# Three score banks, and a new order of exponentials, copies, rotations and maxima, in the attention of a hybrid encoder step

## The reference, cut to what matters

```python
q_lat = jnp.einsum('bthn,chn->bthc', q[..., :MLA_NOPE], lw['w_uk'])
s = jnp.einsum('bqhc,bkc->bhqk', q_lat, ckv) + jnp.einsum('bqhr,bkr->bhqk', q_pe, kpe)
s = s.astype(jnp.float32) * MLA_SCALE
mask = (k_pos[None, :] // CHUNK) <= (q_pos[:, None] // CHUNK)      # CHUNK = 64
s = jnp.where(mask[None, None], s, jnp.finfo(jnp.float32).min)
p = jax.nn.softmax(s, axis=-1).astype(ckv.dtype)
o = jnp.einsum('bhqk,bkc->bqhc', p, ckv)
```

## Time and profile before

| what | value |
|---|---|
| median of three runs | 2607.68 us |
| the profiled execution: its time, its span | 2606.66 us, 2604.8 us |
| TensorE busy | 2562.2 us (98%) |
| VectorE, ScalarE, GpSimd busy | 1644.5, 1137.5, 532.3 us |
| prompt attention, first layer | 617.5 to 700.5 us of the span |
| prompt attention, second layer | 1901.3 to 1984.5 us |
| mean granted TensorE clock | 0.999 |

### The profile page before, as it was taken

One profiled execution on the slowest core, in us unless ns is written; L12 is line 12 of the kernel. 1 busy time (PEld: TensorE's weight loads), 2 busy tenths in 40 slices (PEclk: granted clock), 3 DMA queues, 4 the chain that ended last, 5 costly groups with the idle time before them and its releaser, 6 DMA issues.

```text
span 2604.8 us, 44565 instructions
## 1 busy us (share of the span) xinstructions
PE 2562.2 (98%) x17872; PEld 2446.6 (94%) x17872; DVE 1644.5 (63%) x2566; ACT 1137.5 (44%) x1922; POOL 532.3 (20%) x440
## 2 busy tenths in 40 slices
PE   8999999999999999999999999999999999999998
PEld 8999999996689999999999999999956899999998
DVE  5666575646466866657577574765564757757473
ACT  5343344424654534334454342553165535434253
POOL 0010112103754101011210110121066441101011
PEclk9999999999999999999999999999999999999999
DMA  3322324220025122232313222334100161322231
GB/s 116 91 81 81 97 65 113 73 59 11 20 54 100 49 82 81 84 95 71 108 33 96 83 71 76 89 89 105 27 11 30 46 130 34 97 81 71 85 85 59
DMA packets 369794, 190.73 MB, mean 73 GB/s; under 512 B 38541, under 2 KB 365536, under 8 KB 369630
## 3 DMA queue, kind: packets, MB, share of 16 engines
q1 hardware_dynamic: 365248, 177.89, 25.3%
q0 software_dynamic: 4000, 10.47, 1.8%
q10 hardware_dynamic: 382, 0.14, 0.0%
HBM read 182.53 MB, written 5.93 MB: 72 GB/s over the span
## 4 chain that ended last, share of the span: by engine, by line
PE 90%; DVE 4%; POOL 2%; ACT 2%; issue 1%; DMA 1%; SPq 0%; DVEq 0%; POOLq 0%; ACTq 0%
PE ps L734 27%; PE ps L735 27%; PE ps L736 27%; PE ps L1111 2%; POOL misc L3201 1%; POOL qkc L3204 1%; PE ps L1122 1%; PE ps L1223 1%; DVE at L2696 1%; PE ps L1224 1%; PE ps L1154 0%; PE ps L1245 0%; PE ps L1173 0%; ACT css L1536 0%; PE ps L1236 0%
## 5 line engine op out<-in xcount | busy, mean ns | idle before, releaser
L734 PE MATMUL ps<-xh,w 128*128 128x320 f32 x1920 | 595.3, 310 | 2.8 <-DVE css L2961 2.8
L736 PE MATMUL ps<-xh,w 128*128 128x320 f32 x1920 | 593.5, 309 | 0.0
L735 PE MATMUL ps<-xl,w 128*128 128x320 f32 x1920 | 593.4, 309 | 0.0
L1536 ACT ACTIVATE w<-raw 128x512 fp32r<-128x512 f32 (+3 forms) x372 | 315.8, 861 | 484.2 <-PE ps L736 466.2
L3058 POOL TENSOR_TENSOR hl<-ub,hh 128x640 fp32r<-128x640 f32 x88 | 174.1, 1978 | 1448.4 <-ACT hh L1536 1381.3
L734 PE MATMUL ps<-hh,w 128*128 128x320 f32 x1408 | 438.1, 311 | 3.3 <-DVE ub L2352 1.2
L735 PE MATMUL ps<-hl,w 128*128 128x320 f32 x1408 | 435.2, 309 | 0.0
L736 PE MATMUL ps<-hh,w 128*128 128x320 f32 x1408 | 435.2, 309 | 0.0
L734 PEld LDWEIGHTS ps<-xh,w 128*128 128x128 f32 x1920 | 360.4, 188 | 4.9 <-DVE css L2961 3.2
L735 PEld LDWEIGHTS ps<-xl,w 128*128 128x128 f32 x1920 | 360.4, 188 | 0.3
L736 PEld LDWEIGHTS ps<-xh,w 128*128 128x128 f32 x1920 | 360.4, 188 | 0.0
(11 more groups left out here) (418 smaller groups left out, 4671.2 us busy)
## 6 DMA issues: line engine op xcount, KB each, us to landing
raw<-in_w_ffn_in_dram SPq DMA_DIRECT2D x176, 512.0 KB
raw<-in_w_ffn_out_dram SPq DMA_DIRECT2D x192, 192.0 KB
raw<-in_w_in_dram SPq DMA_DIRECT2D x38, 512.0 KB
raw<-in_w_ffn_out_dram SPq DMA_DIRECT2D x64, 128.0 KB
wraw<-in_w_out_dram SPq DMA_DIRECT2D x8, 512.0 KB
raw<-in_w_out_dram SPq DMA_DIRECT2D x8, 512.0 KB
out_dram<-xio SPq DMA_DIRECT2D x5, 512.0 KB
xin<-in_x_prompt_dram SPq DMA_DIRECT2D x4, 512.0 KB, 7.6
```

Of the source, the lines that this page charges most:

```text
L734: pe.matmul(out, wh, xh, start=first, stop=False, skip_group_check=loose)
L735: pe.matmul(out, wh, xl, start=False, stop=False, skip_group_check=loose)
L736: return pe.matmul(out, wl, xh, start=False, stop=last, skip_group_check=loose)
L1536: return nc.scalar.activation(out, in_, func, **kw)
```

## The change

The scores get a third PSUM bank, taken in the order 3, 4, 2. The latent queries move out of bank 2 into the end of bank 1, and the rotary queries beside them, as two matmuls of 64 columns on different rows instead of one of 128, with two copies on ScalarE instead of one. The scores of a head's tile 3 are made one step earlier, and those of the next head's tile 1 and 2 too; tile 0 of the next head stays where it was. ScalarE does the exponential of tile n + 2 ahead of the copy of tile n + 1, but for each head's step i = 2, where the old order stays. VectorE takes a head's last maximum ahead of the rotation of the next head's second half, which stood before it; the gate steps stay ahead of the maximum of their tile.

```diff
--- before.py
+++ after.py
@@ -597,6 +597,10 @@
         w = 2 * LEVELS[n]
         return ap.rearrange("p (n q) -> p n q", q=w)[:, :, w // 2:w]
 
+    def scores_of(n):
+
+        return PS[:, (3, 4, 2)[n % 3], :]
+
     def level_end(n):
 
         return sum(k <= n for k, _ in LEVEL_STEPS)
@@ -1137,9 +1141,11 @@
             pe.wait_ge(*q_ready.nth(l, 2 * h + 1))
             if h:
                 pe.wait_ge(*ql_sb.nth(l, h - 1))
-            pe.matmul(PS[:, 2, 0:P], WUKT[:, h, :], QT[0:NOPE, h % 2, TP:T], start=True, stop=True)
-            pe.matmul(PS[0:ROPE, 1, HALF:HALF + P], PAIR, QT[NOPE:P, h % 2, TP:T], start=True, stop=True)\
-                .then_inc(ql_ps.sem, 1)
+            pe.matmul(PS[:, 1, HALF:HALF + P], WUKT[:, h, :], QT[0:NOPE, h % 2, TP:T], start=True, stop=True)
+            for e in range(2):
+                mm = pe.matmul(PS[ROPE * e:ROPE * e + ROPE, 1, HALF + P:512], PAIR,
+                               QT[NOPE:P, h % 2, TP + 64 * e:TP + 64 * e + 64], start=True, stop=True)
+            mm.then_inc(ql_ps.sem, 1)
 
         def attend_scores(l, n):
             h, i = divmod(n, PT_)
@@ -1149,9 +1155,11 @@
                 pe.wait_ge(*kt_sb.nth(l, h))
                 if h == 0:
                     pe.wait_ge(*kt_rope.nth(l, 0))
-            if n >= 2:
-                pe.wait_ge(*exp_sb.nth(l, n - 2))
-            pe.matmul(PS[:, 3 + n % 2, 0:(i + 1) * P], QT[:, h % 2, i * P:(i + 1) * P],
+            if n >= 3:
+                pe.wait_ge(*exp_sb.nth(l, n - 3))
+            elif n == 2:
+                pe.wait_ge(*kt_sb.nth(l, 1))
+            pe.matmul(scores_of(n)[:, 0:(i + 1) * P], QT[:, h % 2, i * P:(i + 1) * P],
                       KT[:, h % 2, 0:(i + 1) * P], start=True, stop=True).then_inc(s_ps.sem, 1)
 
         def attend_transpose(l, n):
@@ -1250,6 +1258,7 @@
             mla_prep(l)
             attend_scores(l, 0)
             attend_scores(l, 1)
+            attend_scores(l, 2)
             pe.wait_ge(*cn_sb.nth(l, 0))
             head_queries(l, 1, 0)
             head_latents(l, 0)
@@ -1258,8 +1267,10 @@
                 h, i = divmod(n, PT_)
                 if i == 1 and h + 1 < H:
                     head_queries(l, h + 1, 1)
-                if n + 2 < NT:
+                if n + 2 < NT and i == 2:
                     attend_scores(l, n + 2)
+                if n + 3 < NT and i != 1:
+                    attend_scores(l, n + 3)
                 if i == 0 and h % 2 and h + 1 < H:
                     pair_keys(l, h // 2 + 1)
                 if i == 2 and h + 2 < H:
@@ -1884,9 +1895,11 @@
 
             def latent_queries(h):
                 act.wait_ge(*ql_ps.nth(l, h))
-                run(QLAT[:, :, h, :], PS[:, 2, 0:P].rearrange("p (b t) -> p b t", t=TS), ACT.Copy)
-                run(QPE[0:ROPE, :, h, :], PS[0:ROPE, 1, HALF:HALF + P].rearrange("p (b t) -> p b t", t=TS), ACT.Copy)\
-                    .then_inc(ql_sb.sem, 1)
+                run(QLAT[:, :, h, :], PS[:, 1, HALF:HALF + P].rearrange("p (b t) -> p b t", t=TS), ACT.Copy)
+                for e in range(2):
+                    ins = run(QPE[0:ROPE, 4 * e:4 * e + 4, h, :],
+                              PS[ROPE * e:ROPE * e + ROPE, 1, HALF + P:512].rearrange("p (b t) -> p b t", t=TS), ACT.Copy)
+                ins.then_inc(ql_sb.sem, 1)
 
             def probabilities(n):
                 h, i = divmod(n, PT_)
@@ -1895,7 +1908,7 @@
                     act.wait_ge(*t_ps.nth(l, n - 2))
                 if i == 0 and h > 3 and h % 2 == 0:
                     act.wait_ge(*rs_sb.nth(l, h // 2 - 2))
-                run(PB[:, n % 2, 0:(i + 1) * P], PS[:, 3 + n % 2, 0:(i + 1) * P], ACT.Exp,
+                run(PB[:, n % 2, 0:(i + 1) * P], scores_of(n)[:, 0:(i + 1) * P], ACT.Exp,
                     bias=MX[:, n % 4, 1:2], accum_out=SUMS[:, h // 2 % 2, i, h % 2:h % 2 + 1]).then_inc(exp_sb.sem, 1)
 
             def transposed(n):
@@ -1970,11 +1983,13 @@
                     head_queries(h + 1, 1)
                 if i == 0 and h:
                     latent_queries(h)
+                if n + 2 < NT and i != 2:
+                    probabilities(n + 2)
                 if n + 1 < NT:
                     transposed(n + 1)
                 if n % 8 == 2 and n > 8:
                     pair_rows(n // 8 - 1)
-                if n + 2 < NT:
+                if n + 2 < NT and i == 2:
                     probabilities(n + 2)
                 if i == 0 and h % 2 and h + 1 < H:
                     head_keys(h + 1)
@@ -2657,8 +2672,8 @@
                 i = n % PT_
                 dve.wait_ge(*s_ps.nth(l, n))
 
-                chain.link(V.memset(PS[0:64, 3 + n % 2, i * P + 64:(i + 1) * P], -FAR))
-                V.reduce_max(MX[:, n % 4, 1:2], PS[:, 3 + n % 2, 0:(i + 1) * P], AX_X, negate=True)\
+                chain.link(V.memset(scores_of(n)[0:64, i * P + 64:(i + 1) * P], -FAR))
+                V.reduce_max(MX[:, n % 4, 1:2], scores_of(n)[:, 0:(i + 1) * P], AX_X, negate=True)\
                     .then_inc(nm_sb.sem, 1)
 
             def inverse_sums(pair):
@@ -2787,9 +2802,9 @@
                     gate_ends_exponents()
                 if n == 16:
                     gate_negative()
+                maximum(n)
                 if n % PT_ == PT_ - 1 and n // PT_ + 1 < H:
                     rotated(n // PT_ + 1, 1)
-                maximum(n)
                 if n % PT_ == 0 and n // PT_ + 1 < H:
                     rotated(n // PT_ + 1, 0)
                 if n % 8 == 1 and n > 8:
```

## The result

The changed kernel is slower: 2611.80 us median (2609.59 to 2614.34, 20 runs) against 2607.34 us (2605.45 to 2608.74, 20 runs) on the same chip, a recorded ratio of 1.0019 with a 95% interval of 1.0012 to 1.0025 (the two medians alone give 1.0017). I had forecast 2607.2 us and 2603.2 to 2610.5. The profiled execution took 2609.59 us, its span is 2607.8 us, and its mean granted clock 0.998 (before: 0.999).

The account below looks back on a forecast made before the run. GpSimd's chain from ScalarE's copy qt to the streams' first matmul bounds the stage; two layers at 0.2 us plus 0.1 slack save 0.5, so 2606.2 profiled, 2607.2 us median, range 2603.2 to 2610.5.

Parts of the forecast that it names:

- GpSimd's start: Attention stage: GpSimd's differences start when ScalarE copies qt at n = 5, forecast 0.2 us earlier in each layer.
- the copy of tile 3: ScalarE's copy of tile 3's transposes, ahead of qt: forecast to start at 628.2 instead of 628.75, 0.55 us earlier.
- tile 6's exponential: On ScalarE ahead of qt: forecast 0.55 us earlier, still waiting for its maximum, as it did 1.49 us.
- tile 5's copy: ScalarE's 0.36 us copy, formerly inside the exponential's wait, now behind it; reduces the 0.55 us gain to 0.2.
- the parts without a price: Extra rotary matmuls and copies, and the reorderings: assumed free under waits; could remove up to TensorE's 4.1 idle us.
- GpSimd's chain: From GpSimd's start to the streams' first matmul: 63.2 us, with no step that the change edits.
- wait for kn: TensorE's wait ahead of the streams' first matmul: forecast to grow from nothing visible (first layer) to 2 or 3 us.
- (B): GpSimd's taps fall ahead of VectorE's scans and qt comes earlier: 1.5 to 2.4 us a layer, 2603 to 2604.6; chance 0.15.
- Rival (C): Copies stand behind exponentials awaiting late maxima, delaying GpSimd's second wait: 2616, or 2610.4 at half; chance 0.17 in all.
- The port: GpSimd's first tap against VectorE's scan: tap first gains 1.3 us, scan first loses 0.3; no change taken.
- Rival (A): TensorE's order decides the stage, so its idle time counts: 2591 if all went, 2599.5 with 4.1 us; chance 0.07.
- Rival (D), the clock: TensorE arrives up to 4.1 us early, stands still and the granted clock falls: 2610.6 us; chance 0.06.

Follow-up runs that it names:

- banks_rotation: Changed kernel with the exponential back behind the copy at every step; third bank, earlier scores and last maximum ahead of rotation kept: 2608.27 us.
- section 3: Experiments moving GpSimd's gate-row stores ahead of its last four taps (changed kernel 2611.94 us, kernel before 2606.21), or using the exponential's new place only late.
- taps_out_after: Changed kernel without the second and third convolution tap on GpSimd (8 of 12 taps left out, result differs): 2603.38 us.
- banks_only: Changed kernel with both new orders undone; third score bank, moved latent queries and earlier scores alone: 2611.02 us.
- late_taps_after: Changed kernel, whole computation, GpSimd's tap 1 only behind the second differences, then clears and stores, tap 2, cache loads, tap 3: 2622.19 us.
- tap1_out_after: Changed kernel without tap 1 of the convolution (4 of GpSimd's 12 taps, beside the first gate steps): 2605.03 us.
- filler_after: Changed kernel with four filling matmuls of 256 columns ahead of the transposes at n = 3 to 9: 2613.42 us.
- stores_first_after: Changed kernel with GpSimd's clears of QPE and two gate-row stores ahead of its last four taps: 2611.94 us.
- taps_early_after: Changed kernel, whole computation, with GpSimd's differences and taps 1 and 2 each allowed to begin one head earlier: 2615.70 us.
- late_exponential: Changed kernel with the exponential ahead of the copy only from step n = 15 on: 2608.63 us.
- late_exp_stores_first: Changed kernel with the exponential ahead only from n = 15 on and GpSimd's stores ahead of its last four taps: 2608.66 us.
- banks_exponential: Changed kernel with the last maximum back behind the rotation; banks and exponential ahead of the copy kept: 2616.05 us.
- orders_only: Kernel before, with two score banks and its own score order, plus both new orders (exponential ahead of copy, maximum ahead of rotation): 2620.71 us.
- filler_before: Kernel before with four filling matmuls of 256 columns ahead of the transposes at n = 3 to 9: 2615.71 us.
- stores_first_before: Kernel before with GpSimd's clears and gate-row stores ahead of its last four taps: 2606.21 us.

## Why the prediction was wrong

**What held.** GpSimd's start 0.2 us earlier (20.28 to 20.09 us into the stage). The steps behind it too: the copy of tile 3 was to come 0.55 us earlier and came 0.49 earlier (11.22 to 10.73 into the stage), tile 6's exponential waits 1.60 us where I had left the 1.49, and tile 5's copy of 0.38 us stands behind it, as worked out. In the second layer the first tap was in front of the scan, which I had left open. The extra passes and copies cost nothing measurable in banks_rotation, which has them all.

**What failed: the parts without a price.** The step is "The earlier scores, the exponentials ahead of copies, and the last maximum ahead of the rotation from n = 6 on can remove up to the 4.1 us of TensorE's idle time, but they end in a longer wait for kn, since GpSimd is late." I took GpSimd's chain as fixed at 63.2 us behind its start ("no step of them is one that the change edits"), though its second start hangs on a copy qt in ScalarE's new order. It took 65.7 us in the first layer and 66.5 in the second (66.46 = 86.55 - 20.09), because its second start waits 2.80 and 4.27 us for ScalarE's qt. The wait for kn did not grow to 2 or 3 us; it is not visible in the first layer and 0.19 us in the second. TensorE came no earlier, it came later. One reading in front of that step was too strong as well: "GpSimd has almost none". In the stretch behind 637.8 GpSimd is idle for 62.70 - 56.72 = 6.0 us, more than TensorE's 4.1, though 3.6 of them lie behind its stores. And the lower end of the range does not follow from (B): 2607.7 - 0.1 - 4.8 is 2602.8, not 2603.2.

**Rival (C) had the mechanism, with chance 0.17, but not its price.** The copy behind an exponential behind a late maximum, and the decision at GpSimd's second wait, are as it says; half of its case gave 2610.4, and 2611.8 came. What I had not worked out is that its cover goes away by itself. I read ScalarE's waits for maxima from the kernel before and treated the gate steps' durations as given. They are not: the sum of their 20 instructions over a stage is 14.0 us before, 15.0 and 15.7 after, and 12.1 without the taps beside them. (banks_rotation has 15.8 and 15.3 and loses nothing measurable, so it takes both the longer gate step and the exponential in front of the copy.) Nor is (C)'s last link right. The stage isn't later because the stores are; it ends as late with the stores moved ahead (section 3).

**The port: right event, wrong question.** I asked who is first in one pair, tap or scan, and took it as GpSimd's gain or loss of 1.3 us. GpSimd's first tap did get 1.16 us shorter. But where a tap is first a gate step loses (the scan 0.4 us, the product of 4x640 1.3, the copy 1.2), and behind the new order a gate step is on the path (maximum, exponential, copy, transposes, qt) while a tap isn't: GpSimd's four first taps end 18.4 us behind their start after the change and 18.6 before, so GpSimd as a whole gained 0.2 us by it. The Trainium skill ("SBUF — State Buffer", "SBUF: two separate sides") says that the shared port is an exclusive lock for a whole instruction. The runs agree as far as they go. In the second layer the product begins at 1927.43, inside an instruction of GpSimd that ends at 1928.79, and ends 0.67 us behind that end (it takes 0.76 alone); the 4x3 copy, which has one input, ends 0.03 us behind the end of the one beside it (1942.44). Tap 1 left out, or behind them, brings them back to 0.76 and 0.16 us. No run took the port apart from other ways in which the two could hinder each other.

**Rival (A) lives inside the result.** TensorE's own order did end the stage within 0.3 to 0.7 us of GpSimd's chain (83.21 and 82.86 us without the eight taps, against 83.48 and 83.57), as I had read it from the slack of 0.2 us. The gain that the change could have is 1.9 us a stage (81.57 against 83.48), not 4.1 or 8.3.

**Rival (D), the clock**, came at another place: in the versions with three banks it begins 18 to 21 us into the stage (14 times), 31 to 32 (3 times) or 41 (once, behind an earlier one), and not near 700 us. What it costs can be read only from the two stages of one kernel, one with a fall and one without: 85.65 and 84.35 (banks_rotation), 83.02 and 81.57 (taps_out_after), 85.10 and 84.31 (banks_only), 83.25 and 81.22 (late_taps_after), 83.94 and 81.71 (tap1_out_after, 6.8 us at 0.50 instead of 3.4). These give 0.8 to 2.2 us. The other pairs spread further: 0.3 (filler_after), 0.5 (stores_first_after, again 6.8 us at 0.50), 0.8 to 1.0 (late_exponential, late_exp_stores_first, banks_exponential) and 2.6 (taps_early_after, 10.2 us at 0.50), and without any fall the two layers of a kernel already differ by 0.1 to 0.4. The profiled executions show a fall in no stage of the three versions with the orders of before and no fillers (6 stages), in 17 of 30 stages of the versions with three banks, and in both stages of orders_only and of filler_before, 39 to 40 us into them. Both stages of the changed kernel's profile have one: they are 0.5 and 1.3 us above the one stage of that order without a fall (85.29). What decides is only partly the order. stores_first_after runs the same order up to that place, TensorE was busy for 0.92 and 0.89 us of the same two windows, which have 0.99 and 0.89 above, and its clock stayed at 1.00:

```profile
634.00:636.00 2.00, 0.92 (x11) 0.73 (x11) 1.26 (x3) 2.00 (x5) 0.00 (x0) 1.00 0.01 4
636.00:638.00 2.00, 0.89 (x8) 0.71 (x5) 0.90 (x2) 1.97 (x6) 0.62 (x1) 1.00 0.00 0
```

**What stays open.** How the loss divides. In the profiled executions the 5.3 us of the two stages are 3.5 at full clock (85.29 against 83.48 and 83.57) and 1.8 of falls, but the first figure rests on a single stage, of stores_first_after, and I have no run that holds the clock. A second reading is the mean granted clock of each run. At 0.998, 52 runs of the kernel before (of the 124 that ran beside the experiments, on other chips too) have a median of 2608.3 us and 5 runs of the changed kernel 2610.6; at 0.997, 3 have 2610.3 and 11 have 2612.4. So 2.1 to 2.3 of the 4.5 us are there at an equal clock, and the rest goes with a lower one: 15 of the 20 changed runs are at 0.997 or below, and 3 of those 124. That lower clock may itself come from the order, so it is no separate cause.

Does the clock alone make the differences between the versions? A fit over all these runs gives 1.4 us for each 0.001 of the mean clock within a kernel. By this estimate, at one clock banks_rotation is level with the kernel before, banks_only and the changed kernel are 2.0 us above it and banks_exponential 7.1, and tap1_out_after is 6.1 below the changed kernel. So the order and the taps keep most of what the medians gave them.

Other ends are open too. Why the three banks alone, without either order, cost 3.4 us was not taken further. And no version that computes the whole result beats the kernel before by a measurable margin: stores_first_before is 1.5 us below it with an interval that holds 1. One that keeps the taps off the gate steps and the cache's loads ahead of them wasn't tried.

## What to carry to other kernels

Before an instruction that can always run is put behind one that waits, find what the wait hangs on, and whether that work's duration depends on what runs beside it. The measured durations of two engines that hold each other up are not constants: shift one and the other changes, and here the stretch on the critical chain cost more than the other engine saved. When an ordering loses, take out the neighbour that isn't part of it (here four taps of GpSimd): it told in one run what four re-orderings had not.

## What was not expected of the hardware

A copy of 4x3 numbers took 0.16 us alone and 1.39 us with an instruction of a GpSimd tap beside it (128x640, 1.89 us), and a 4x640 product 0.76 and 2.03. So a tiny operation of VectorE can stand for most of a large one of GpSimd that began before it. Not every meeting does this: a 4x640 product took 0.81 us beside a tap at 654.37. And the granted clock fell to 0.50 for 3.4 us with no gap of TensorE longer than 1.3 us ahead of it in the first layer, in some executions and stages and not in others with the same order; a stage with a fall was 0.3 to 2.6 us longer than the other stage of its kernel.
